# Loading the gate and up matrices of a mixture-of-experts layer as pairs of half-partition transfers with 16 KB runs

## The reference, cut to what matters

```python
def ec_moe(h, router_w, router_b, w_gate, w_up, w_down):
    ...
    cap = CAPACITY_FACTOR * S // N_EXPERTS
    aff = jax.nn.softmax(logits, axis=-1)
    gate, idx = lax.top_k(jnp.swapaxes(aff, 1, 2), cap)
    xg = h[bidx, idx]
    hid = jax.nn.silu(jnp.einsum("becd,edf->becf", xg, w_gate)) * jnp.einsum("becd,edf->becf", xg, w_up)
    y = jnp.einsum("becf,efd->becd", hid, w_down) * gate[..., None].astype(h.dtype)
    return jnp.zeros_like(h).at[bidx, idx].add(y)
```

## Time and profile before

| | us |
|---|---|
| median of 3 runs | 1898.81 |
| lowest, highest | 1891.2, 1898.91 |
| the profiled execution | 1903.91 |
| its span | 1902.1 |
| PE busy | 1480.0 (78%) |
| DVE, ACT, POOL busy | 434.6, 231.8, 25.7 |
| main DMA queue (q1) | 101040 packets, 623.76 MB |
| mean DMA rate over the span | 335 GB/s |

### The profile page before, as it was taken

How to read it: one execution, slowest core, us unless ns; L and a number is a source line. 1 busy time by engine, 2 the same in 40 slices (tenths; PEclk the granted TensorE clock), 3 DMA queues, 4 the chain that set the end, 5 groups by cost and what they waited for, 6 DMA issues and landing times.

```text
span 1902.1 us, 26117 instructions
## 1 busy us (share of the span) xinstructions
PE 1480.0 (78%) x11264; PEld 757.4 (40%) x11264; DVE 434.6 (23%) x965; ACT 231.8 (12%) x466; POOL 25.7 (1%) x46
## 2 busy tenths in 40 slices
PE   5989877666776667989766667666799985899996
PEld 3834432323322234545322323222346652555553
DVE  1462311104000022443100000000125453311112
ACT  2111100001000020332000000000022222100001
POOL 1000000000000000000000000000020000000000
PEclk8988877878777878769877777776799997899998
DMA  9697999999999973856999999999942302599995
GB/s 376 217 362 292 417 421 421 421 421 421 421 421 421 421 285 111 330 201 243 413 420 421 421 421 421 421 421 421 417 156 100 132 13 100 199 422 420 421 421 218
DMA packets 104812, 638.03 MB, mean 335 GB/s; under 512 B 10524, under 2 KB 10524, under 8 KB 42240
## 3 DMA queue, kind: packets, MB, share of 16 engines
q1 hardware_dynamic: 101040, 623.76, 80.7%
q0 software_dynamic: 3664, 12.64, 1.9%
HBM read 635.30 MB, written 1.96 MB: 335 GB/s over the span
## 4 chain that ended last, share of the span: by engine, by line
DMA 47%; PE 43%; DVE 5%; ACT 3%; issue 1%; SPq 0%; DVEq 0%; ACTq 0%
PE ps L1832 41%; DMA ring<-in_moe_w_up 29%; DMA ring<-in_moe_w_down 15%; PE ps L1835 2%; DMA ring<-in_ada_w 2%; ACT work L2127 1%; DMA ring<-in_moe_w 1%; DVE x L2345 1%; DVE tmp L2343 1%; ACT xn L2127 0%; ACT L2127 0%; SPq L279 0%; ACT hT L2127 0%; ACT tmp L2127 0%; DVE work L619 0%
## 5 line engine op out<-in xcount | busy, mean ns | idle before, releaser
L1832 PE MATMUL ps<-ring,work 128*32 128x256 f32 (+3 forms) x7760 | 831.9, 480 | 289.7 <-DMA ring<-in_moe_w_up 105.9
L1832 PEld LDWEIGHTS ps<-ring,work 128*32 128x32 f32 (+2 forms) x7760 | 342.4, 134 | 759.1 <-issue 226.2
L2127 ACT ACTIVATE work<-ps 128x256 f32<-128x256 f32 (+3 forms) x188 | 89.2, 479 | 1288.1 <-PE ps L1832 1016.3
L1832 PE MATMUL ps<-work 32*128 32x256 f32 (+6 forms) x1034 | 147.7, 480 | 17.5 <-ACT work L2127 15.6
L2478 DVE TENSOR_TENSOR work<-work,ps 128x256 f32<-128x256 f32 x32 | 13.5, 422 | 595.2 <-ACT work L2127 595.2
L1832 PEld LDWEIGHTS ps<-work 32*128 32x128 f32 (+3 forms) x1034 | 89.8, 221 | 73.6 <-issue 51.3
L1832 PE MATMUL ps<-ring,condT 128*32 128x512 f32 x576 | 84.4, 721 | 21.5 <-DMA ring<-in_ada_w 13.6
L1832 PE MATMUL ps<-ring,hT 128*128 128x512 f32 (+1 forms) x224 | 97.1, 597 | 2.4 <-issue 1.3
L1835 PE MATMUL ps<-const,work 128*128 128x128 f32 (+1 forms) x394 | 67.3, 303 | 23.4 <-ACT work L2127 7.3
L1832 PE MATMUL ps<-work,xn 128*128 128x128 f32 (+2 forms) x416 | 69.3, 320 | 6.8 <-DVE work L1670 6.8
L1835 PEld LDWEIGHTS ps<-const,work 128*128 128x128 f32 (+1 forms) x394 | 50.4, 169 | 58.8 <-issue 25.0
(11 more groups left out here) (294 smaller groups left out, 695.5 us busy)
## 6 DMA issues: line engine op xcount, KB each, us to landing
ring<-in_moe_w_gate SPq DMA_DIRECT2D x128, 1024.0 KB, 17.8
ring<-in_moe_w_up SPq DMA_DIRECT2D x128, 1024.0 KB, 18.1
ring<-in_moe_w_down SPq DMA_DIRECT2D x128, 1024.0 KB, 18.0
ring<-in_moe_w SPq DMA_DIRECT2D x102, 1024.0 KB, 11.2
ring<-in_ada_w SPq DMA_DIRECT2D x72, 1024.0 KB, 8.8
ring<-in_w_in SPq DMA_DIRECT2D x10, 1024.0 KB, 19.6
ring<-in_fc_w_in SPq DMA_DIRECT2D x6, 1024.0 KB, 27.7
ring<-in_attn_w_qkv SPq DMA_DIRECT2D x6, 1024.0 KB, 18.1
```

The costliest lines, as they stand in the source:

```text
L1832: return pe.matmul(out, lhsT, rhs, start=start, stop=stop, skip_group_check=True)
L2127: return nc.scalar.activation(out, in_, f, **kw)
```

## The change

The gate and up pieces of the first block's experts are loaded two at a time. Piece n and piece n + 1 (n even) are neighbouring slots, and `pair(n)` sees them as one tile of 16 KB a partition. Two DMAs fill it: the first writes both slots on partitions 0 to 63, the second both slots on partitions 64 to 127, 1 MB each, in runs of 16 KB. Each raises the semaphore of one of the two slots, and TensorE waits for both before it uses the pair. The loader waits once for both slots (`place_free` of n + 1) and then issues both. The order becomes two pieces of gate, two of up, two of gate, two of up; `piece_used` still rises once in 16 matmuls. Pieces of the down matrix, of all other weights and of the second block are loaded as before.

```diff
+        def pair(n):
+            return ring[:, n % SLOTS:n % SLOTS + 2, :].rearrange("p a (k f) -> p (a k) f", k=2)
+
+        def load_pair(sp, n, src):
+            for half in range(2):
+                r = slice(64 * half, 64 * half + 64)
+                sp.dma_start(pair(n)[r], src[r]).then_inc(S(f"loaded{(n + half) % SLOTS}"), 16)
...
-                        order = [w[s][:, 0, kp // 2, 2 * (kp % 2):2 * (kp % 2) + 2, :] for kp in range(4) for s in range(2)]
-                        order += [down[:, 0, kp] for kp in range(4)]
-                        for j, src in enumerate(order):
-                            n = n0 + 12 * u + j
+                        for q in range(2):
+                            for s in range(2):
+                                n = n0 + 12 * u + 4 * q + 2 * s
+                                place_free(sp, n + 1, BODY * i)
+                                load_pair(sp, n, w[s][:, 0, q])
+                        for kp in range(4):
+                            n = n0 + 12 * u + 8 + kp
                             place_free(sp, n, BODY * i)
-                            load(sp, n, src)
+                            load(sp, n, down[:, 0, kp])
...
-                    for kp in range(4):
+                    for q in range(2):
...
                         for s in range(2):
-                            loaded(pe, n + 2 * kp + s)
-                            w = slot(n + 2 * kp + s).rearrange("p (k f) -> p k f", k=2)
-                            for kk in range(2):
+                            m = n + 4 * q + 2 * s
+                            loaded(pe, m)
+                            loaded(pe, m + 1)
+                            for kk in range(4):
                                 for j in range(4):
                                     last = mm(ps[32 * j:32 * j + 32, 4 + s, 0:SEQ],
-                                              xe[:, c % 2, 2 * kp + kk, CAP * u:CAP * u + CAP],
-                                              w[:, kk, SEQ * j:SEQ * j + SEQ],
-                                              kp == 0 and kk == 0, kp == 3 and kk == 1)
-                            last.then_inc(S("piece_used"), 1)
+                                              xe[:, c % 2, 4 * q + kk, CAP * u:CAP * u + CAP],
+                                              pair(m)[:, kk, SEQ * j:SEQ * j + SEQ],
+                                              q == 0 and kk == 0, q == 1 and kk == 3)
+                                if kk % 2:
+                                    last.then_inc(S("piece_used"), 1)
```

More of the change, by code:

```diff
@@ L2050, in experts @@
                         pe.wait_ge(S("spread_ready"), layer * E + e)
-                    for kp in range(4):
-                        if e == 0 and kp == 0:
+                    for q in range(2):
+                        if e == 0 and q == 0:
                             pe.wait_ge(S("xe_dve"), 28 * layer + 4)
-                        if e == 0 and kp == 2:
+                        if e == 0 and q == 1:
                             pe.wait_ge(S("xe_act"), 4 * layer + 4)
-                        if e and u == 0 and kp == 0:
+                        if e and u == 0 and q == 0:
                             pe.wait_ge(S("xe_dve"), 28 * layer + 4 + 8 * c)
                         for s in range(2):
-                            loaded(pe, n + 2 * kp + s)
-                            w = slot(n + 2 * kp + s).rearrange("p (k f) -> p k f", k=2)
-                            for kk in range(2):
+                            m = n + 4 * q + 2 * s
+                            loaded(pe, m)
+                            loaded(pe, m + 1)
+                            for kk in range(4):
                                 for j in range(4):
                                     last = mm(ps[32 * j:32 * j + 32, 4 + s, 0:SEQ],
-                                              xe[:, c % 2, 2 * kp + kk, CAP * u:CAP * u + CAP],
-                                              w[:, kk, SEQ * j:SEQ * j + SEQ],
-                                              kp == 0 and kk == 0, kp == 3 and kk == 1)
-                            last.then_inc(S("piece_used"), 1)
+                                              xe[:, c % 2, 4 * q + kk, CAP * u:CAP * u + CAP],
[3 more added lines that the diff above has]
+                                    last.then_inc(S("piece_used"), 1)
                     if e == 1:
```

## The result

The changed kernel takes 2703.97 us (median of 4 runs, 2679.47 to 2720.24) against 1897.38 us before (now also of 4 runs), or +807 us. The ratio, 1.4217 with a 95% interval of 1.4112 to 1.4321, is taken without the slowest run of the changed kernel, whose time lay over 1.5% above the quickest. The profiled execution is the quickest of the four, 2679.47 us, with a span of 2677.7.

The account below looks back on a forecast made before the run. The prediction took the arrival of expert weights by DMA as the bound. To the profiled 1903.9 us it added 504.6 for half-partition transfers, giving 2408.5, less 5.1 for the median: 2403 us, range 1885 to 2541.

Parts of the forecast that it names:

- Bound: First block's expert stages: arrival of weights sets the end; the touched gate and up pieces are 637.6 us of DMA time.
- Reordering: Expert loop: two gate pieces, then two up pieces, instead of taking turns; same bytes and matmuls, cost nothing.
- coarser freeing: Loader SP waits for a pair's second buffer before issuing either half; hidden by the queue, cost nothing; 248 us excluded.
- coarser waiting: TensorE waits for both halves, 32 matmuls left after the last bytes instead of 16; taken as 0, at most 4 us.
- granted clock: TensorE's work per expert, doubled for a lower clock, would be 41.6 us, covered by 45.7 us of loading; nothing added.
- The run of 16 KB: Gate and up loads: half the packets, 9.1 ns fixed cost per run, 36 ns saved per piece, -9.4 us in all.
- Rival B: A 16 KB run is carried as two 8 KB packets, so with free halves nothing is won: 1899 us; chance 0.14.
- Half of the partitions: Gate and up transfers to 64 partitions run at 235 GB/s: 4.462 us a piece, +1.971 us each, +504.6 us in all.
- The down pieces should keep their price: Sign expected in the new profile: the experts' down pieces, unchanged, still take 2.49 us each.
- the upper end, 2541: Top of the forecast range in us: exactly halved path rate plus 4 us at the layer ends.
- A: Rival for gate and up loads: half transfers cost nothing and the long runs pay, 1889.4 us; chance 0.24.
- C: Rival for gate and up loads: both halves go at about 210 GB/s, half of 421, +637.6 us, 2536 us; chance 0.22.

Follow-up runs that it names:

- halves alone: Changed kernel with its down pieces also loaded in pairs by two transfers of half the partitions each, in runs of 8 KB: 2723.02 us, one run.

## Why the prediction was right in direction and wrong in size

**Bound.** Right. The arrival of weights set the end before and after; with the DMA rate down to 258 and 214 GB/s, the chain has 60% of DMA instead of 47%.

**Reordering, coarser freeing, coarser waiting.** Costed at nothing, and shown: 0.999 with all three alone. TensorE at a granted clock of 0.61 to 0.65 was also covered, as argued: its 32 matmuls take 3.6 us and it waited 4.8 us or more for each of the pairs shown.

**The run of 16 KB.** The working from 4 KB and 8 KB gave 613.5 ns for such a run per engine; it took 614 and 612 over all 128 and over even and odd partitions. Nine microseconds were expected, 13.4 are measured (1897.4 - 1884.0), with an interval from 9 to 18. Rival B, that a run would be carried as two packets, falls by the packet count.

**Half of the partitions.** This is the step that failed, in two ways. First its size, 4.46 us a piece: I took 235 GB/s, the row of the sixteen small `rpb_rows` loads, as the likeliest and half the rate as the end. With halves alone, engines in step, the rate was 218 to 220, 4.8 us a piece. In the first part a 16 KB packet took 1157 ns on average in layer 0 and 1195 in layer 1 (1310 to 1630 us), and an engine has four of them in a piece: 4.63 and 4.78 us. Why the small loads came to 235 was not tried; they differ in their runs of 256 bytes and in passing at a DMA share of 0.46.

Second, a term put at nothing: "The down pieces should keep their price." They did not, and from the start. In the first part their packets took 378 ns on average (372 in layer 1) and not 314, so a down piece took 3.0 us and not 2.5. Eight pieces of 4.63 and four of 3.02 are 49.1 us; from the rate, 12.58 MB at 258 GB/s, an expert takes 48.8, where the prediction had 45.7. Were it so to the end, the kernel would have taken 1897 + 32 x (48.8 - 29.9) = 2502 us. So 99 of the 301 us between prediction and result are in the first part's price, about half of them in the down pieces: 4 x 0.53 = 2.1 us an expert in layer 0, beside 8 x 0.17 = 1.4 in gate and up, and 1.9 beside 2.6 in layer 1.

The other 200 us (2704 - 2502) are the second part, and they are why even the upper end, 2541, was passed. There an expert took 12.58 MB / 214 GB/s = 58.8 us at a share of 0.90. The records show what sets this pace: the one late engine. From last landing to last landing a gate or up piece took 4.33 us and a down piece 6.01, and 8 x 4.33 + 4 x 6.01 = 58.7 us. The other 15 wait for it. At 700 us in layer 0, for example, a gate pair landed on 15 engines by 681.3 us and on the last at 698.8; TensorE then used it, and the issue into its two buffers went out at 702.8. About 16 of the 32 experts ran like this, 10 us each: 160 of the 177 us by which the profiled execution, 2679, exceeds 2502. The late engine's down packets pass while the others are at the next expert's halves: its four down pieces after 700 us landed between 711.9 and 730.0, the others' next gate and up pieces from 709.8 on. That the two collide is the likely reason, but no run isolates it, and 6.01 us is more than the 4.8 us that a down piece by halves takes in the kernel of halves alone. With a look-ahead of four or six pieces the fall to 214 was absent. That one engine falls behind is seen in several kernels; why it does, and why several do when the upper half goes first, stays open.

**Rivals.** A, free halves, is what happens with even and odd partitions. For partitions 0 to 63 and 64 to 127 its argument, that engines drift apart and use both halves, is real but small: it shows plainly only in the kernel of halves alone, 300 GB/s for 130 us. C, an exact half, was nearest, for gate and up pieces, and was given 0.22 because "the engines never stay in perfect step". For hundreds of microseconds they do: over 99% of the packets of the kernel of halves alone between 240 and 600 us took over 1.5 times their duration in whole transfers. C had the down pieces at their old price too.

The Trainium skill, page "SBUF — State Buffer", section "Door 1: The DMA port swizzle", has 218 GB/s as the limit for partitions 0 to 63, and the runs agree with it to the digit (218 and 220). Its map also assigns even partitions to all 16 ports, which the runs with even partitions bear out. The prediction gives the 6% for two concurrent transfers under the same section; it stands on the same page under "Can I just issue two DMAs to hit both halves?". The sum by the figure of 218, 2493 us, would have been nearer than mine and still 211 us short, for want of the down pieces' price and the late engine.

## What to carry to other kernels

Before splitting a bulk load by partitions, ask which partitions each part takes: lower and upper halves alone ran at 218 GB/s, even and odd, with whole down pieces between them, at the full 425. A longer run per partition is worth little and is to be had without a split: 2 MB over 128 partitions in 16 KB runs gave 0.7%. And when transfers of unequal rate share one ring, look at the spread of an issue's 16 landings: in the slow half of each layer here the pace was that of the last engine, and the look-ahead bounded how far it could fall behind (3.6, 13.7 and 35.5 us with four, six and eight pieces). The pieces that a change leaves alone can change their price too, when they share the engines with those that it touches.

## What the hardware showed that was not expected

One DMA engine of 16 fell about 20 us behind the other 15 and stayed there for hundreds of microseconds, and its down pieces took 6.0 us each where they had taken 2.5. Half transfers alone got quicker as their engines fell out of step, from 220 to 300 GB/s. And allowing the loader fewer pieces ahead, four instead of eight, made the changed kernel quicker: 2620 us in its one run, under the lowest of the changed kernel's four, 2679.
